# A branch's product moved to GpSimd, its transposes to block moves and VectorE, and two weight strips interleaved

## The reference, cut to what matters

```python
z = h @ w_in[l]                       # columns: u, v, cq, ckv, kr, gates ga and gb
u = gelu(a_u)                         # (256, 1024)
v = layer_norm(gelu(a_v))
mixed = einsum('gts,bcsgd->bctgd', tril(w_s), vc) + b_s      # 8 groups of 128 channels
y_a = (u * mixed) @ gm_w_proj[l]      # "pa": the branch's projection
y_b = attention(...) @ mla_w_proj[l]  # "pb": 16 heads, worked in 8 pairs
merged = sigmoid(ga) * y_a + sigmoid(gb) * y_b
x = x + merged @ w_out[l]             # "wo"
x = x + ffn(rms_norm(x))              # dense in layer 0, 2 of 8 experts in layer 1
```

## Time and profile before

| | us |
|---|---|
| median of 3 runs | 1415.64 |
| lowest and highest | 1414.63, 1416.27 |
| the profiled execution | 1414.55 |
| its span in the profile | 1412.70 |
| TensorE busy | 1404.8 |
| VectorE busy | 1166.5 |
| ScalarE busy | 950.6 |
| GpSimd busy | 170.0 |

### The profile page before, as it was taken

One profiled execution on the slowest core, in us unless ns is written; L12 is line 12 of the kernel. 1 busy time (PEld: TensorE's weight loads), 2 busy tenths in 40 slices (PEclk: granted clock), 3 DMA queues, 4 the chain that ended last, 5 costly groups with the idle time before them and its releaser, 6 DMA issues.

```text
span 1412.7 us, 19105 instructions
## 1 busy us (share of the span) xinstructions
PE 1404.8 (99%) x6575; PEld 1160.5 (82%) x6575; DVE 1166.5 (83%) x1196; ACT 950.6 (67%) x968; POOL 170.0 (12%) x302
## 2 busy tenths in 40 slices
PE   9999999999999999999999999999999999999998
PEld 7888778888888888788888888888888888888886
DVE  6998766676557899667989898898998988989987
ACT  6678645445445677644777787777877777778775
POOL 2031003476500050000300000000000000000010
PEclk9999999999999999999999999999999999999999
DMA  9476549976666483558899999999999999999996
GB/s 339 163 220 204 179 150 332 297 231 201 205 216 193 162 244 125 205 170 322 311 361 410 364 395 408 384 373 408 356 410 384 375 408 364 395 387 394 409 347 211
DMA packets 171587, 424.32 MB, mean 300 GB/s; under 512 B 19388, under 2 KB 50744, under 8 KB 171496
## 3 DMA queue, kind: packets, MB, share of 16 engines
q1 hardware_dynamic: 157128, 393.42, 76.7%
q0 software_dynamic: 13328, 26.16, 6.2%
q10 hardware_dynamic: 1040, 3.68, 0.6%
HBM read 398.20 MB, written 15.81 MB: 293 GB/s over the span
## 4 chain that ended last, share of the span: by engine, by line
PE 98%; DVE 1%; DMA 0%; ACT 0%; issue 0%; SPq 0%; DVEq 0%
PE ps L619 91%; PE ps L1186 1%; PE ps L1045 1%; PE ps L1054 1%; PE ps L924 1%; PE ps L1043 1%; PE ps L1029 1%; PE ps L1002 0%; PE ps L968 0%; DMA raw<-in_w_in 0%; PE ps L1027 0%; PE ps L1178 0%; PE ps L1223 0%; PE ps L985 0%; ACT act_hi L1329 0%
## 5 line engine op out<-in xcount | busy, mean ns | idle before, releaser
L554 DVE TENSOR_TENSOR w_lo<-raw,w_hi 128x2048 fp32r<-128x2048 f32 (+3 forms) x184 | 383.8, 2093 | 78.6 <-ACT w_hi L549 77.1
L549 ACT ACTIVATE w_hi<-raw 128x2048 fp32r<-128x2048 f32 (+3 forms) x184 | 322.3, 1758 | 121.4 <-PE ps L619 99.2
L619 PE MATMUL ps<-w_hi,act_hi 128*128 128x512 f32 (+1 forms) x1264 | 332.4, 391 | 0.4 <-DVE w_hi L1795 0.3
L619 PE MATMUL ps<-w_hi,act_lo 128*128 128x512 f32 (+1 forms) x1264 | 328.5, 387 | 0.0
L619 PE MATMUL ps<-w_lo,act_hi 128*128 128x512 f32 (+1 forms) x1264 | 326.8, 387 | 0.0
L619 PEld LDWEIGHTS ps<-w_lo,act_hi 128*128 128x128 f32 x1264 | 235.7, 188 | 48.2
L619 PEld LDWEIGHTS ps<-w_hi,act_lo 128*128 128x128 f32 x1264 | 235.5, 188 | 48.1
L619 PEld LDWEIGHTS ps<-w_hi,act_hi 128*128 128x128 f32 x1264 | 233.1, 188 | 46.7 <-ACT act_hi L1329 1.0
L554 DVE TENSOR_TENSOR w_lo<-raw_more,w_hi 128x2048 fp32r<-128x2048 f32 (+1 forms) x96 | 201.8, 2110 | 31.4 <-ACT w_hi L549 31.4
L549 ACT ACTIVATE w_hi<-raw_more 128x2048 fp32r<-128x2048 f32 (+1 forms) x96 | 169.9, 1775 | 56.0 <-PE ps L619 51.7
L554 DVE TENSOR_TENSOR w_lo<-raw_low,w_hi 128x2048 fp32r<-128x2048 f32 (+1 forms) x64 | 137.5, 2155 | 11.7 <-ACT w_hi L549 10.9
(11 more groups left out here) (294 smaller groups left out, 1353.3 us busy)
## 6 DMA issues: line engine op xcount, KB each, us to landing
raw<-in_moe_w_gu SPq DMA_DIRECT2D x96, 512.0 KB, 11.8
raw_more<-in_moe_w_down SPq DMA_DIRECT2D x80, 512.0 KB, 9.5
raw<-in_w_in SPq DMA_DIRECT2D x66, 512.0 KB, 5.4
raw_low<-in_moe_w_gu SPq DMA_DIRECT2D x64, 512.0 KB, 12.1
raw_more<-in_moe_w_gu SPq DMA_DIRECT2D x64, 512.0 KB, 12.6
raw<-in_moe_w_gu SPq DMA_DIRECT2D x48, 384.0 KB, 8.7
raw<-in_dense_w_gu SPq DMA_DIRECT2D x34, 512.0 KB, 5.5
raw_lent<-in_moe_w_gu SPq DMA_DIRECT2D x32, 512.0 KB, 11.2
```

Source lines behind the costliest of these rows:

```text
L549: nc.scalar.activation(w_hi[:, self.split_slot(j), 0:n], self.raw(j)[:, 0:n], ACT.Copy).then_inc(self.hi, 1)
L554: nc.vector.tensor_tensor(w_lo[:, c, 0:n], self.raw(j)[:, 0:n], w_hi[:, c, 0:n].bitcast(F32), ALU.subtract).then_inc(self.lo, 1)
L619: return nc.tensor.matmul(dst, a, b, start=start and n == 0, stop=stop and n == 2)
```

## The change

For both halves of the branch, in both layers:

- GpSimd makes the product: it scales `u_buf` by the norm's scale (two instructions of 128x512), then multiplies by `vbuf` (two more).
- `mix_tokens` on ScalarE writes its result so that within each half the 32-column blocks of one partition group lie together, which takes a wait for both banks before the first write.
- GpSimd's queue then moves 16 blocks of the half back into `u_buf`, 32 KB each.
- VectorE transposes the moved half in one instruction (`a_blocks`) into a part of `kb`, whose keys have been moved by then.
- ScalarE copies it to `t1_hi` (`a_hi`), VectorE subtracts it to `t1_lo` (`a_lo`).
- TensorE's `a_turns` is gone. It waits for `a_hi` ahead of the first pass of a pa chunk and for `a_lo` ahead of the second.
- The chunks pa 0/0, pa 0/4, ga 1/0, ga 1/4 now run as pa 0/0, ga 1/0, pa 0/4, ga 1/4, and the steps between them are put in another order.
- Some semaphores of the router are merged into `routed_by_pe` and `routed_by_act`, counted in the order in which they were given.

The diff, with the renaming of the router's semaphores cut:

```diff
         plan.append(("blocks", l, "q", 1))
-        mul(l, "u", 0, 4, [("u_arg", l, 0), split("split_hi"), ("blocks", l, "k", 0), ("u_gelu", l, 0), ("branch", l, 0)],
+        mul(l, "u", 0, 4, [("u_arg", l, 0), split("split_hi"), ("blocks", l, "k", 0), ("u_gelu", l, 0)],
             split=False)
         mul(l, "u", 1, 0, [*slot(1, exps=False), ("split_lo", l, len(chunks) - 2), split("split_hi")], split=False)
         mul(l, "u", 1, 4, [("u_square", l, 1), *slot(2, exps=False), ("u_arg", l, 1), ("softmax", l, 1)], split=False,
-            inside=[(2, ("a_turns", l, 0)), (2, ("softmax", l, 0)), (2, ("last_q", l, "q", 1)),
+            inside=[(2, ("softmax", l, 0)), (2, ("last_q", l, "q", 1)),
                     (5, ("split_lo", l, len(chunks) - 2)), (5, split())])
         mul(l, "gb", 1, 0, [("values", l, 0), split("split_hi"), *slot(3, values=False, exps=False), ("u_gelu", l, 1),
-                            ("branch", l, 1), ("blocks", l, "k", 1)], split=False, inside=[(4, ("u_tanh", l, 1))])
+                            ("a_blocks", l, 0), ("blocks", l, "k", 1), ("a_lo", l, 0)], split=False, inside=[(4, ("u_tanh", l, 1))])
         mul(l, "gb", 1, 4, [("values", l, 1), ("split_lo", l, len(chunks) - 2), *slot(4, values=False, exps=False), split("split_lo"), ("softmax", l, 3), evac("gb", 1)], split=False,
-            inside=[(2, ("exps", l, 2)), (5, ("a_turns", l, 1)), (7, ("norm_probs", l, 2)),
+            inside=[(2, ("exps", l, 2)), (5, ("a_hi", l, 0)), (7, ("norm_probs", l, 2)),
                     (7, split("split_hi"))])
-        mul(l, "pa", 0, 0, [*slot(5, exps=False), split("split_lo"), ("softmax", l, 4)],
-            inside=[(4, split("split_hi"))])
-        mul(l, "pa", 0, 4, [*slot(6), evac("pa", 0)])
-        mul(l, "ga", 1, 0, [*slot(7)])
+        mul(l, "pa", 0, 0, [*slot(5, exps=False), split("split_lo"), ("softmax", l, 4), ("a_blocks", l, 1),
+                            ("split_hi", l, len(chunks)), ("a_hi", l, 1)], split=False, inside=[(4, split("split_hi"))])
+        mul(l, "ga", 1, 0, [("values", l, 3), ("a_lo", l, 1), *slot(6, values=False, exps=False),
+                            ("split_lo", l, len(chunks) - 1), ("softmax", l, 5)])
+        mul(l, "pa", 0, 4, [*slot(7), evac("pa", 0)])
         mul(l, "ga", 1, 4, [*slot(8), evac("ga", 1)])
...
         kb = sb("kb", [P, TT, DG, H, 32], F32, mixer)
+        branch_moved = u_buf[:].rearrange("p j t n -> p j (t n)").rearrange("p j (t b k i) -> p j t b k i", t=TT, b=4, k=4)
+        branch_turned = kb[:].rearrange("p t g h d -> p (t g h d)")[:, 4 * STRIP:6 * STRIP]
+        branch_by_tile = branch_turned.rearrange("p (t b k i) -> p t b k i", t=TT, b=4, k=4)
         vv = sb("vv", [P, TT, H, DV], F32, mixer)
...
 
+
+        BY_BLOCKS = 2
+
+        def branch_by_block(j):
+
+            return vbuf[:, :, j * STRIP:(j + 1) * STRIP].rearrange("p t (c k i) -> p t c k i", c=4, k=4)
...
                     "ukv": lambda: last_turn["latent_turns", l, 1],
-                    "pa": lambda: last_turn["a_turns", l, half],
+                    "pa": lambda: None if half < BY_BLOCKS else last_turn["a_turns", l, half],
                     "pb": lambda: last_turn["values", l, 4 * half + 3],
...
                 move_heads(k_blocks[1], kb, slice(8, H), k_moved[1])
+                for j in range(BY_BLOCKS):
+                    wait_strip_read(pool, strip_at[l, "u", j])
+                    wait_turn_read(pool, last_turn["mix_tokens", l, j])
+                    wait_turn_read(pool, last_turn["mix_tokens", l, j] - 1)
+                    for t in range(TT):
+                        u = u_buf[:, j, t, :]
+                        op = nc.gpsimd.tensor_scalar(u, u, mix_scale[:, ONE, t:t + 1], None, ALU.mult)
+                    op.then_inc(branch_a, 1)
+                    pool.wait_ge(branch_a, 4 * l + 2 * j + 1)
+                    for t in range(TT):
+                        v, u = branch_by_block(j)[:, t], u_buf[:, j, t, :].rearrange("p (k c i) -> p c k i", c=4, k=4)
+                        op = nc.gpsimd.tensor_tensor(v, u, v, ALU.mult)
+                    op.then_inc(branch_a, 1)
+                    pool.wait_ge(branch_a, 4 * l + 2 * j + 2)
+                    for b in range(4):
+                        for c in range(4):
+                            pool.dma_start(branch_moved[32 * c:32 * c + 32, j, :, b, :, :],
+                                           branch_by_block(j)[32 * b:32 * b + 32, :, c, :, :]).then_inc(a_moved[j], 16)
                 if not l:
 
                     pool.wait_ge(merged_b, 2)
                     zeros = ws_raw[:].rearrange("p g t -> p (g t)")
-                    nc.gpsimd.memset(zeros, 0.0).then_inc(zeroed, 1)
-                    pool.wait_ge(zeroed, 1)
+                    nc.gpsimd.memset(zeros, 0.0).then_inc(ident_ready, 1)
+                    pool.wait_ge(ident_ready, 4)
                     for e in range(E):
...
                     tiles_first = (what, j, k0) == ("wo", 1, 4)
+                    blocked = what == "pa" and not j and k0 // 4 < BY_BLOCKS
                     if not first:
+                        if blocked:
+                            pe.wait_ge(a_hi, BY_BLOCKS * l + k0 // 4 + 1)
                         if operand is not None:
...
                                 ring.take_lo(pe, 0, c)
+                        elif p == 1 and not cell and blocked:
+                            pe.wait_ge(a_lo, BY_BLOCKS * l + k0 // 4 + 1)
                         elif p == 1 and not cell and operand is not None:
...
                             gg = 4 * step[2] + 2 * b + g
-                            op = nc.scalar.activation(vbuf[:, :, gg * P:(gg + 1) * P],
-                                                      ps[:, 4 + bb % 2, g * S:(g + 1) * S].rearrange(
-                                                          "p (t d) -> p t d", t=TT),
-                                                      ACT.Identity, bias=b_sp[:, l, gg:gg + 1], scale=0.5)
+                            if step[2] < BY_BLOCKS:
+                                if not b and not g:
+                                    act.wait_ge(turn_done, bb + 2)
+                                dst, src = branch_by_block(step[2])[:, :, :, 2 * b + g, :], "p (t c i) -> p t c i"
+                                src = ps[:, 4 + bb % 2, g * S:(g + 1) * S].rearrange(src, t=TT, c=4)
+                            else:
+                                dst = vbuf[:, :, gg * P:(gg + 1) * P]
+                                src = ps[:, 4 + bb % 2, g * S:(g + 1) * S].rearrange("p (t d) -> p t d", t=TT)
+                            op = nc.scalar.activation(dst, src, ACT.Identity, bias=b_sp[:, l, gg:gg + 1], scale=0.5)
                         op.then_inc(turn_free[bb % 2], 1)
+                elif kind == "a_hi":
+                    j = step[2]
+                    act.wait_ge(a_turned, BY_BLOCKS * l + j + 1)
+                    for t in range(TT):
+                        op = copy(t1_hi[:, 4 * j:4 * j + 4, t * P:(t + 1) * P].rearrange("p k (b i) -> p k b i", b=4),
+                                  branch_by_tile[:, t].rearrange("p b k i -> p k b i"))
+                    op.then_inc(a_hi, 1)
                 elif kind == "values":
...
                     nc.vector.transpose(part, part).then_inc(done, 1)
-                elif kind == "branch":
-
+                elif kind == "a_blocks":
                     j = step[2]
-                    cols = slice(j * STRIP, (j + 1) * STRIP)
-                    wait_strip_read(dve, strip_at[l, "u", j])
-                    wait_turn_read(dve, last_turn["mix_tokens", l, j])
-                    wait_turn_read(dve, last_turn["mix_tokens", l, j] - 1)
+                    dve.wait_ge(a_moved[j], 16 * 16 * (l + 1))
+                    if not j:
+                        dve.wait_ge(k_moved[1], 16 * 4 * DG * (l + 1))
+                    nc.vector.transpose(branch_turned, u_buf[:, j].rearrange("p t n -> p (t n)")).then_inc(a_turned, 1)
+                elif kind == "a_lo":
+                    j = step[2]
+                    dve.wait_ge(a_hi, BY_BLOCKS * l + j + 1)
                     for t in range(TT):
-                        op = stt(vbuf[:, t, cols], u_buf[:, j, t, :], mix_scale[:, ONE, t:t + 1], vbuf[:, t, cols],
-                                 ALU.mult, ALU.mult)
-                    op.then_inc(branch_a, 1)
+                        k, cols = slice(4 * j, 4 * j + 4), slice(t * P, (t + 1) * P)
+                        op = tt(t1_lo[:, k, cols].rearrange("p k (b i) -> p k b i", b=4),
+                                branch_by_tile[:, t].rearrange("p b k i -> p k b i"),
+                                t1_hi[:, k, cols].bitcast(F32).rearrange("p k (b i) -> p k b i", b=4), ALU.subtract)
+                    op.then_inc(a_lo, 1)
                 elif kind in ("u_arg", "u_gelu"):
```

(8 more changed lines are left out.)

32 lines of the change are left out of this document (15 added, 17 removed).

## The result

| | before | after |
|---|---|---|
| median of 6 runs each, us | 1415.94 | 1421.36 |
| lowest and highest, us | 1414.63, 1416.35 | 1420.03, 1422.49 |
| the profiled execution, us | 1414.55 | 1420.51 |
| its span, us | 1412.70 | 1418.80 |

The ratio of after to before is 1.0039, with an interval of 1.0029 to 1.0049: 5.4 us slower. 3.3 us less were forecast, and the range ended at 1416.5.

The account below looks back on a forecast made before the run. TensorE was taken as the bound, busy 99% of the span, with VectorE right behind. 3.92 us of transposes less 0.6 of contention gave 3.3 us less, 1412.3 us from a median of 1415.64; range 1411.0 to 1416.5.

Parts of the forecast that it names:

- TensorE loses 3.92 us of transposes: Transposes of the gMLP product (line 924): 2 x 8 per layer removed, 1.96 us per layer, 3.92 us in all.
- Nothing is added on TensorE: TensorE, pa and ga strips: the alternation runs the same 96 matmuls in another order, so no added time.
- TensorE goes through the rest of the layer without a wait that a lead could run into: TensorE after the removed transposes: ground for excluding the rival that TensorE gains nothing because the end was set elsewhere.
- GpSimd's four products, 3.5 us with bounds of 2.2 and 4.6: GpSimd after `u_gelu`: two one-input and two two-input products of 128x512 take 3.5 us, between 2.2 and 4.6.
- my upper row's 1.16: Upper bound for one 128x512 GpSimd product: 1.16 us, scaled by columns from a 128x128 select of 0.289 us.
- 16 moves, 8.6 us, landing 3.1 to 5.9 us later: GpSimd's block moves of half 0: 0.540 us each, 8.6 us, landed at 134.7 to 137.5, hidden with 0.6 to 3.4 to spare.
- the slower rival: Half 0's moves land late, at 140.9 with upper bounds: 2.6 us stall per layer, 1416.9 us; slower by over 2.8: 0.13.
- VectorE at `a_blocks` 0 at 138.1, pair 2 done at 143.95, 0.2 us to spare: Layer 0: VectorE reaches half 0's transpose at 138.1, pair 2's probabilities are done at 143.95, TensorE asks at 144.18.
- Contention, 0.5 us of VectorE per layer: VectorE waiting for GpSimd products on SBUF: 0.5 us per layer, 0.3 beyond the spare 0.2, 0.6 in both layers.
- contention takes the gain: VectorE waits twice for a 1.16 us product per layer: 0 to 2.8 us faster; 0.35 together with slightly late moves.
- The rival of late moves: VectorE stands at `a_blocks` 0; each us beyond 138.3 costs one per layer, 1416.9 us with upper bounds; 0.13 for clearly slower.
- Half 1's transpose and subtraction, ScalarE, the interleaving, the merged semaphores: nothing: Remaining parts, each costed at nothing: half 1's VectorE work in the pa and ga strips, ScalarE's copies, chunk order, semaphores.

Follow-up runs that it names:

- no_product: Changed kernel without GpSimd's four scaling and product instructions per half, only the block moves: 1413.69 us, ratio to before 0.9992.
- no_moves: Changed kernel with the product kept and the 16 block moves per half left out: 1420.04 us, ratio to before 1.0036.
- order_only: Kernel before with only the chunk order pa 0/0, ga 1/0, pa 0/4, ga 1/4: 1415.57 us, ratio to before 1.0003.
- act_scale: Changed kernel with the scale applied by ScalarE in mix_tokens, GpSimd making only the two products: 1413.78 us, ratio to before 0.9991.
- act_scale_order: ScalarE scaling, GpSimd products only, plus a_lo 0 moved behind pair 1's values and the high split behind pair 2's, against the changed kernel: 1412.22 us.
- early_split: As act_scale_order, with VectorE's low weight split put ahead of the maximum of pair 0: 1415.45 us, ratio to before 0.9997.

## Why the prediction was wrong, point by point

- **"TensorE loses 3.92 us of transposes."** Right in what it takes away; the gain without a product is 1.3 us (`no_product`). The step that failed is "Nothing is added on TensorE", with the later "TensorE goes through the rest of the layer without a wait that a lead could run into". The transposes had covered other waits. Before, the third pass of u 1/0 began 0.33 us after the low split it needs was done (122.09 + 2.28 = 124.37, and 124.70 in TensorE's timeline); with 0.87 us of transposes gone it starts when the split is done (124.48 and 124.53): a wait of 0.3 to 0.4 us. Behind pair 3's scores the change left ScalarE's order as it was, with `bt_hi` behind the evacuation of gb 1 and the weights' copy. TensorE used to come just in time for the `bt_lo` that follows (its six transposes took 1.07 us in place of 0.82). In `no_product` it comes 1.6 us earlier and `bt_lo` only 0.95 (153.76 against 154.71): a wait of 0.69 us. And for pair 1 there had been no spare time at all; VectorE's and TensorE's timelines of the kernel before:

```profile
135.53 0.68 DVE L1977 TENSOR_TENSOR sq<-sq,soft 128x512 f32<-128x512 f32 x1
```

```profile
136.27 1.11 PE L1054 MATMUL ps<-consts,sq 128*128 128x128 f32 x6
```

The probabilities are done at 136.21 and taken up at 136.27. The view that tells all this, each of TensorE's starts against the end of what it needs, I made for pair 2 only.
- **GpSimd's four products, 3.5 us with bounds of 2.2 and 4.6.** Measured 7.2 us from the end of `u_gelu` to the last product. Undisturbed they take 2 x 1.56 + 2 x 1.28 = 5.7 us, outside both bounds: both rows that I scaled from were of a `select`, another operation. The order was wrong too: the one-input scaling by a column of scalars is the dearer one. The Trainium skill (GPSIMD Engine Reference, "Elementwise — side-by-side cycle accounting") gives 2.6 cycles per column, 1.1 us by an estimate for the product; the traces have 1.28, and my upper row's 1.16 was a little nearer. No row here lets me say what makes the scaling dearer.
- **16 moves, 8.6 us, landing 3.1 to 5.9 us later.** 8.56 us and 5.0 us after the last issue: right. But the start was wrong by the 3.7 us of the products, so they landed at 140.9, which is the number of the slower rival, with another cause than its upper bounds.
- **VectorE at `a_blocks` 0 at 138.1, pair 2 done at 143.95, 0.2 us to spare.** With the product out, 138.63 and 144.39. VectorE did come early out of the splits, by 1.2 us (130.19 against 131.37), but then stood idle 0.47 us for TensorE's scores of pair 2, and of the lead 0.7 us was left at `a_blocks` 0. So there was no spare time: TensorE took up the probabilities at 144.44, and its way from the scores of pair 3 to those of pair 4 grew by 0.26 us. That VectorE is the second bound was right, and it is why every stretch of VectorE is paid.
- **Contention, 0.5 us of VectorE per layer.** This is the step that failed most. Measured 0.70 + 1.08 at the normalisation of pair 0 in both layers, and then 1.21 at `a_lo` in layer 0 and 0.85 at the normalisation of pair 2 in layer 1: 3.0 and 2.6 us. The rival "contention takes the gain" allowed two waits of 1.16 us, 2.3; and GpSimd was stretched as well, which delayed the moves. `no_moves` against `no_product` puts 6.4 us on it, where the sum had 0.6; what lateness adds on top is 0.4 by the ratios, within their intervals. I had taken from the earlier trace rows that VectorE lost nothing; there VectorE had been first. The Trainium skill (SBUF — State Buffer, "SBUF: two separate sides") says that either engine excludes the other for a whole instruction, whichever starts first. This case's traces agree for two-input VectorE against the two-input product, in both orders: GpSimd's product waits for the split's end at 124.48, VectorE's normalisation for the product's end at 127.06. The rule stood beside my sum with the right sign; I gave it a small weight because one row showed one order.
- **The rival of late moves.** Its mechanism is there (0.97 and 1.44 us of idle time at `a_blocks` 0 in the two layers), but it came together with contention and not instead of it, and cost little besides. The two were priced as alternatives, and here they have one cause: a product that is late and stretched.
- **What neither had:** the granted clock in layer 1, 1.6 us.
- **Half 1's transpose and subtraction, ScalarE, the interleaving, the merged semaphores: nothing.** `order_only` confirms the interleaving. For the others no wait shows up, and they weren't tried by themselves.

What stays open: layer 0's waits of 0.4, 0.53, 2.16 and 0.68 us less the 1.96 us of transposes make 1.8 of its 2.3 us; the rest lies in pieces of 0.1 to 0.25 us between groups, which I didn't assign. Why the clock fell in one layer and not in the other isn't settled either.

## What to carry to other kernels

Before instructions are taken off the bounding engine, list for each of its next starts how long what it needs has been ready: about the smallest of these is all that comes out there, unless what it waits for comes earlier too. Before work is moved to GpSimd, lay its instructions over VectorE's timeline: a two-input product beside VectorE's two-input instructions costs both engines, beside its reads of PSUM it is free, and the window that is free can be short (here 120.0 to 122.6 us). Two rivals that start from the same delay aren't alternatives: price them together.

## What the runs showed of the hardware that I had not expected

- A one-input `TENSOR_SCALAR` of GpSimd with a scalar per partition takes 1.56 us for 128x512 (1555 to 1576 ns over eight), a two-input `TENSOR_TENSOR` 1.28 us where nothing holds it, and up to 2.63 us in the changed kernel.
- The one-input scaling held nobody up: VectorE's split of two SBUF inputs kept its 2.29 us beside it, and it kept its 1.56. Wherever the two met, the scaling had started first; the other order was not seen. The exclusion that the rule above states for any GpSimd instruction that reads SBUF was seen only with the two-input product here (and with the `select` of the earlier trace rows).
- Even an instruction of four columns waits: VectorE's 128x4 took 0.16 us alone, and in layer 0 it took 0.42 (`act_scale`), 0.58 (`act_scale_order`) and 1.28 us (`early_split`) beside a product of GpSimd's.
- After a wait of 2.27 us of TensorE the granted clock was 0.51 for some 3 us in layer 1, and after one of 2.16 us in layer 0 it stayed at 1.00. In `no_moves` the wait was 1.8 us in both layers and the table above shows no such loss.
